# Latent attention: scores of both heads in row groups, value product in one piece, five turned pieces

## The chip, the core and the metric

The kernel runs on one NeuronCore of a Trainium2 chip. The metric is device time in microseconds (us) of one execution, the median of several. TensorE (PE) multiplies and transposes into PSUM, eight banks of 512 f32 columns; VectorE (DVE) and ScalarE (ACT) read PSUM and write SBUF, GpSimd (POOL) works in SBUF, SyncE (SP) issues DMAs. Each engine follows its own list of instructions; semaphores join them.

## What is computed

Two transformer blocks. The change touches the second attention of the first block, the latent one. Eight heads (H_B = 8), each with 64 own query and key numbers and 32 rotary ones; the rotary keys kr are the same for all heads. 1024 queries, in tiles of 128, meet 1280 keys (256 of the context, 1024 own).

```python
def mla_attend(qn, qr, kn, kr, v):
    s = (jnp.einsum('bqhd,bkhd->bhqk', qn, kn) + jnp.einsum('bqhr,bkr->bhqk', qr, kr)) * MLA_SCALE
    p = jax.nn.softmax(s, axis=-1)
    return jnp.einsum('bhqk,bkhd->bqhd', p, v)
```

All of it is in f32.

## The kernel before

`first_attention` runs the stages one after the other: a window attention (`attend_pairs`, line 710 scores, 733 value products, 690 transposes), then `project_latent`, then `attend_latent`. The window attention already scores its two heads from 64-row halves of the array in turn.

`project_latent` goes through a list `uses` of products, one PSUM bank each, eight banks in turn: rotary queries (four banks, rotated by VectorE), values (10), rotary keys (3), keys (12), queries (8), rotary queries turned (8). A bank of keys or queries holds two heads, 64 rows each; ScalarE copies one half, VectorE the other, since the two heads' operands are laid out differently: `kT_b` and `qT_b` have 96 rows for an even head (own 0 to 63, rotary 64 to 95) and 128 for an odd one (rotary 0 to 31, zeros, own 64 to 127). Rotary keys are copied four times over, once for each pair of heads.

`attend_latent` has 64 steps, a head and a tile of 128 queries each; two steps are a pair (`Pair`, 32 of them). A step needs three score matmuls (512, 512 and 256 columns over all 1280 keys), a maximum (956), an exponential with sum (981), a reciprocal and a scaling (951, 952), ten transposes in pieces of 4, 4 and 2 (897), each piece copied out of PSUM by ScalarE (974), VectorE (961), ScalarE (985), and half of a pair's value product (911), whose result VectorE copies (965). Two heads' scores lie in PSUM at once, at columns 0 and 1280, up to bank 5; pieces take banks 5 and 6 in turn, the product bank 7. The order on each engine is written out: TensorE scores two steps ahead, and puts one part of a step's scores, a piece, the other part, a piece, half a value product and the last piece behind one another. Each wait is on a count of a semaphore.

SyncE loads `w_out` in two halves, the second when 16 pairs are mixed; GpSimd scales them.

Of the kernel before, what the change touches and what calls it, by code (L numbers as in the profile page):

```python
# [476 lines left out]
def project_latent(c, k, kr4, q_rope):  # L477
# [9 lines left out]
    by_act, by_dve = [], []  # L487
    for kind, *at in uses:
        by_act.append((by_act[-1] if by_act else 0) + (kind != "rotate" and (kind != "value" or at[0] % 2 == 0)))
        by_dve.append((by_dve[-1] if by_dve else 0) + (kind != "rotate" and (kind != "value" or at[0] % 2 == 1)))  # L490
# [3 lines left out]

    with nc.Block(no_gpsimd_drain=True) as block:  # L495
        @block.gpsimd
        def _(pool):
            nc.gpsimd.memset(q_rope[:, :, :, 0, 32:64], 0.0).then_inc(spread, 1)
            nc.gpsimd.memset(kr4[:, :, 32:64], 0.0).then_inc(spread, 1)
            for at in (0, 64):  # L500
                nc.gpsimd.tensor_copy(kr4[:, :, at:at + ROPE], k.kr_key[:, :, :]).then_inc(spread, 1)

        @block.tensor
        def _(pe):
            pe.wait_ge(k.up_in["q"], 16)
            for n, (kind, *at) in enumerate(uses):
                if n >= 8:
                    if uses[n - 8][0] == "rotate":
                        pe.wait_ge(rotated, uses[n - 8][1] + 2)
                    else:  # L510
                        pe.wait_ge(act_out, by_act[n - 8])
                        pe.wait_ge(dve_out, by_dve[n - 8])
# [5 lines left out]
                elif kind == "key_rope":  # L518
                    pe.wait_ge(spread, 4)
                    a, b = at[0]  # L520
                    for t in range(a // P, b // P):
                        last = nc.tensor.transpose(bank(n)[0:96, P * t - a:P * t - a + P], kr4[:, t, :], k.ident[:, :])
# [4 lines left out]
                elif kind == "query_rope":  # L527
                    i, a = at
                    pe.wait_ge(rotated, a // P + 4)
                    for t in range(4):  # L530
                        last = nc.tensor.transpose(bank(n)[0:96, P * t:P * t + P],
                                                   q_rope[:, a // P + t, i, :, :].rearrange("p s n -> p (s n)")[:, 0:96], k.ident[:, :])
# [11 lines left out]
        @block.scalar  # L544
        def _(act):
            for n, (kind, *at) in enumerate(uses):
                if kind == "rotate" or kind == "value" and at[0] % 2:
                    continue
                act.wait_ge(made, n + 1)
                if kind == "key_rope":  # L550
                    a, b = at[0]
                    src = bank(n)[0:64, 0:b - a].unsqueeze(1).to_broadcast([64, PAIRS, b - a])
                    ins = nc.scalar.activation(k.kT_b[0:64, 1:HB:2, a:b], src, ACT.Identity)
                elif kind == "query":
                    i, a = at
                    ins = nc.scalar.activation(k.qT_b[0:64, 2 * i, a:a + BANK], bank(n)[0:64, :], ACT.Identity, scale=SCALE)
                elif kind == "query_rope":
                    i, a = at
                    ins = nc.scalar.activation(k.qT_b[0:64, 2 * i + 1, a:a + BANK], bank(n)[0:64, :], ACT.Identity, scale=SCALE)
                elif kind == "key":  # L560
                    i, (a, b) = at
                    ins = nc.scalar.activation(k.kT_b[0:64, 2 * i, a:b], bank(n)[0:64, 0:b - a], ACT.Identity)
                else:
                    act.wait_ge(spread, 4)
                    ins = nc.scalar.activation(k.v_b[:, at[0], :], bank(n), ACT.Identity)
                ins.then_inc(act_out, 1)

        @block.vector
        def _(dve):
            step = Chain(dve, link)  # L570

            def rotate(n, t):
# [9 lines left out]
                for s in range(2):  # L582
# [3 lines left out]
                nc.vector.tensor_tensor(q_rope[:, t, :, :, 0:ROPE], out.rearrange("p (i s e) -> p i s e", i=PAIRS, s=2),  # L586
                                        k.tmp[:, 0:256].rearrange("p (i s e) -> p i s e", i=PAIRS, s=2), ALU.add).then_inc(rotated, 1)

            for n, (kind, *at) in enumerate(uses):
                if kind == "value" and at[0] % 2 == 0:  # L590
                    continue
                dve.wait_ge(made, n + 1)
                if kind == "rotate":
                    for t in (at[0], at[0] + 1):
                        rotate(n, t)
                    continue
                if kind == "key_rope":
                    a, b = at[0]
                    src = bank(n)[64:96, 0:b - a].unsqueeze(1).to_broadcast([32, PAIRS, b - a])
                    ins = nc.vector.tensor_copy(k.kT_b[64:96, 0:HB:2, a:b], src)  # L600
                elif kind == "query":
                    i, a = at
                    ins = nc.vector.tensor_scalar(k.qT_b[64:128, 2 * i + 1, a:a + BANK], bank(n)[64:128, :], SCALE, None, ALU.mult)
                elif kind == "query_rope":
                    i, a = at
                    ins = nc.vector.tensor_scalar(k.qT_b[64:96, 2 * i, a:a + BANK], bank(n)[64:96, :], SCALE, None, ALU.mult)
                elif kind == "key":
                    i, (a, b) = at
                    ins = nc.vector.tensor_copy(k.kT_b[64:128, 2 * i + 1, a:b], bank(n)[64:128, 0:b - a])
                else:  # L610
                    dve.wait_ge(spread, 4)
                    ins = nc.vector.tensor_copy(k.v_b[:, at[0], :], bank(n))
                ins.then_inc(dve_out, 1)
# [220 lines left out]
def attend_latent(c, k, name, heads, bufs, d):  # L834
# [6 lines left out]
    n, W, HALF = 2 * len(heads), NK * P, NK // 2  # L841
    TURN = 5

    def scores(u):
        return c.ps[:, W * (u % 2):W * (u % 2) + W]

    def cuts(u):
        at = W * (u % 2)
        edges = [at] + [b for b in range(0, 8 * BANK, BANK) if at < b < at + W] + [at + W]
        cuts = [(a - at, b - at) for a, b in zip(edges, edges[1:])]  # L850
        return (cuts[:2], cuts[2:]) if u % 2 == 0 else (cuts[1:], cuts[:1])

    def product(p):
        return c.bank(7, P)

    PART = ((0, 4), (4, 4), (8, 2))

    def turn_bank(u, i):
        at = BANK * (TURN + (3 * u + i) % 2)
        return c.ps[:, at:at + P * PART[i][1]]  # L860

    def turned_out(eng, u, i):
        if i == 1:
            eng.wait_ge(out_dve, u + 1)
        else:
            eng.wait_ge(out_act, 2 * u + (1 if i == 0 else 2))

    def place(u, i):
        a, m = PART[i]
        return probT[:, (u // 2) % 2, u % 2, P * a:P * (a + m)]  # L870

    with nc.Block(no_gpsimd_drain=True) as block:
        @block.sync
        def _(sp):
            sp.dma_start(k.w_out[0], d["w_out"][0]).then_inc(k.w_out_in[0], 16)
            sp.wait_ge(mixed, n // 4)
            sp.dma_start(k.w_out[1], d["w_out"][1]).then_inc(k.w_out_in[1], 16)
# [12 lines left out]
        def _(pe):  # L890
            def turn(u, i):
                g = 3 * u + i
                if g >= 2:
                    turned_out(pe, (g - 2) // 3, (g - 2) % 3)
                a, m = PART[i]
                for j in range(m):
                    last = nc.tensor.transpose(turn_bank(u, i)[:, P * j:P * j + P], prob[:, u % 3, P * (a + j):P * (a + j) + P],  # L897
                                               k.ident[:, :])
                last.then_inc(turned, 1)

            def mix(p, half):
                out = product(p)
                if half == 0:
                    for u in (2 * p, 2 * p + 1):
                        turned_out(pe, u, 1)
                        turned_out(pe, u, 2)
                    if p:
                        pe.wait_ge(taken, p)
                for j in range(HALF * half, HALF * half + HALF):
                    for e in range(2):  # L910
                        last = nc.tensor.matmul(out[64 * e:64 * e + 64, :], heads[p].values[e][j],
                                                probT[:, p % 2, e, P * j:P * j + P], start=j == 0, stop=j == NK - 1,
                                                skip_group_check=True)
                if half == 1:
                    last.then_inc(mixed, 1)

            def score(u, part):
                for a, b in cuts(u)[part]:
                    last = nc.tensor.matmul(scores(u)[:, a:b], heads[u // 2].q[u % 2], heads[u // 2].keys[u % 2][:, a:b],  # L919
                                            start=True, stop=True, skip_group_check=True)  # L920
                return last

            for s in range(-2, n + 2):
                u = s + 2
# [2968 lines left out]
```

## Time and profile before

| | us |
|---|---|
| median of 3 runs (3193.18 to 3194.04) | 3193.26 |
| profiled execution | 3194.05 |
| its span | 3192.3 |
| first attention | 240 to 384 |
| latent projections | 384 to 457 |
| latent attention | 457 to 763.5 |
| TensorE busy | 3034.3 |
| mean granted TensorE clock | 0.978 |

An f32 matmul appears in the profile as two instructions with a weight load each, a transpose as one. The recorded length of an instruction of TensorE reaches past the start of the next, so lengths are not prices: the price of one is the distance from its start to the next one's. The stages follow one another without overlap.

### The profile page before, as it was taken

To read this page: it belongs to the slowest core of one execution; us is meant where nothing else is said; L and a number is where in the kernel's file an instruction comes from. 1 tells how busy PE (TensorE), PEld (TensorE's weight loads), DVE (VectorE), ACT (ScalarE), POOL (GpSimd) and SP (SyncE) were. 2 spreads that over 40 slices of the span, in tenths; PEclk is the share of its full clock that TensorE was granted. 3 is DMA by queue.
4 is the path that set the end of the run, shared out by engine and by line. 5 is a ranking of instruction groups with operands and counts; after the bars stand their busy time and mean duration, and the time that the engine had idled before them with its cause. 6 is when DMAs were issued, how large, how long until landed. Compare 5 with 4: busy or idle time off the path is not lost. (4 is left out here: it accounts for less than half of the span.)

```text
span 3192.3 us, 36679 instructions
## 1 busy us (share of the span) xinstructions
PE 3034.3 (95%) x14372; PEld 1715.9 (54%) x14372; DVE 1539.7 (48%) x2538; ACT 808.6 (25%) x1656; POOL 836.3 (26%) x654
## 2 busy tenths in 40 slices
PE   7999999999959999799999999999999999999999
PEld 3456746665424444344456657444445666665444
DVE  2445547776451111524322465314758777775234
ACT  3226534443211111412212026211112222221001
POOL 0004401002000110023032115312616665551323
PEclk9999999999979999899999999999999999999999
DMA  7210000002197986500000130012211122117443
GB/s 298 79 53 29 1 27 1 28 1 82 72 377 290 339 333 215 199 28 36 33 21 29 54 139 2 34 40 79 109 50 66 53 79 80 73 46 290 161 131 135
DMA packets 72315, 334.54 MB, mean 105 GB/s; under 512 B 10960, under 2 KB 12497, under 8 KB 58321
## 3 DMA queue, kind: packets, MB, share of 16 engines
q1 hardware_dynamic: 67536, 315.42, 26.0%
q0 software_dynamic: 4608, 16.78, 2.1%
q8 instruction: 115, 1.88, 0.2%
q14 instruction: 56, 0.45, 0.0%
HBM read 283.92 MB, written 48.23 MB: 104 GB/s over the span
## 5 line engine op out<-in xcount | busy, mean ns | idle before, releaser
L3444 PE MATMUL banks<-down_ring,down_sums 128*128 128x512 f32 x440 | 191.1, 597 | 4.2 <-DVE down_ring L3471 4.2
L919 PE MATMUL banks<-kT_b,qT_b_and_w_out 128*128 128x512 f32 (+3 forms) x384 | 161.9, 532 | 4.3 <-PEq L495 2.5
L3146 PE MATMUL banks<-hT,ffn_raw 128*128 128x512 f32 x352 | 157.6, 601 | 2.4 <-PEq L2632 1.3
L329 PE MATMUL banks<-w_in,hT 128*128 128x512 f32 (+1 forms) x384 | 157.1, 567 | 1.2 <-PEq L157 1.2
L3262 DVE SCALAR_TENSOR_TENSOR ffn_acc<-ffn_u,s_ffn_taps,ffn_acc 128x1023 f32<-128x1023 f32 x88 | 132.5, 1516 | 30.4 <-ACT ffn_acc L3199 28.8
L803 POOL TENSOR_TENSOR prob<-prob,softmax_columns 128x640 f32<-128x640 f32 (+1 forms) x64 | 75.4, 1199 | 263.7 <-DVE softmax_columns L759 263.7
L3444 PEld LDWEIGHTS banks<-down_ring,down_sums 128*128 128x128 f32 x440 | 84.1, 191 | 110.9 <-issue 103.4
L1867 PE MATMUL banks<-hT,side_ring 128*128 128x512 f32 x256 | 126.6, 614 | 1.3 <-PEq L2419 1.3
L1514 PE MATMUL banks<-expert_wg,expert_xT 128*128 128x512 f32 x256 | 114.9, 603 | 2.3 <-ACT expert_xT L1551 1.7
L1593 DVE TENSOR_TENSOR expert_h<-banks,expert_silu 128x512 f32<-128x512 f32 x16 | 11.1, 691 | 219.4 <-ACT expert_silu L1560 219.4
L329 PEld LDWEIGHTS banks<-w_in,hT 128*128 128x128 f32 x384 | 71.9, 190 | 77.9 <-issue 77.9
L1530 PE MATMUL banks<-expert_wd,expert_hT 128*128 128x512 f32 x256 | 112.6, 592 | 1.2 <-DVE expert_y L1585 1.2
L1514 PE MATMUL banks<-expert_wu,expert_xT 128*128 128x512 f32 x256 | 112.5, 592 | 0.0
L956 DVE TENSOR_REDUCE softmax_columns_b<-banks 128x1 f32<-128x1280 f32 x64 | 95.4, 1490 | 35.3 <-PE banks L919 35.3
L3146 PEld LDWEIGHTS banks<-hT,ffn_raw 128*128 128x128 f32 x352 | 67.8, 193 | 79.8 <-issue 76.8
L981 ACT ACTIVATE prob_b<-banks,softmax_columns_b 128x1280 f32<-128x1280 f32 x64 | 85.0, 1327 | 99.7 <-DVE softmax_columns_b L956 99.7
L1491 POOL DMA_INDIRECT expert_sums<-expert_y,idxT x16 | 25.3, 1582 | 319.6 <-DVE expert_y L1585 319.6
L897 PE MATMUL banks<-ident,prob_b 128*128 128x128 f32 x640 | 104.6, 278 | 0.9 <-ACT probT_b L985 0.4
L897 PEld LDWEIGHTS banks<-ident,prob_b 128*128 128x128 f32 x640 | 76.4, 141 | 52.0 <-issue 44.8
L3164 PE MATMUL banks<-ffn_split_rows,ffn_split_sums 128*128 128x256 f32 x352 | 84.0, 380 | 2.6 <-ACT ffn_chain L3189 2.5
L3471 DVE TENSOR_TENSOR down_ring<-down_ring 128x512 f32<-128x512 f32 x49 | 39.4, 810 | 96.3 <-DMA down_ring<-in_w_down 95.8
L2742 PE MATMUL banks<-hT,gate_ring 128*128 128x512 f32 x192 | 85.1, 592 | 0.7 <-PEq L673 0.7
(636 smaller groups left out, 6122.8 us busy)
## 6 DMA issues: line engine op xcount, KB each, us to landing
down_ring<-in_w_down SPq DMA_DIRECT2D x132, 256.0 KB, 2.9
expert_wg<-in_w_gate SPq DMA_DIRECT2D x16, 2048.0 KB, 15.4
expert_wu<-in_w_up SPq DMA_DIRECT2D x16, 2048.0 KB, 20.7
expert_wd<-in_w_down SPq DMA_DIRECT2D x16, 2048.0 KB, 8.7
ffn_raw<-in_w_ffn SPq DMA_DIRECT2D x22, 1024.0 KB, 6.4
wmod_slab<-in_w_mod SPq DMA_DIRECT2D x6, 2048.0 KB, 8.1
act_rows<-ffn_acc SPq DMA_DIRECT2D x22, 512.0 KB, 2.7
act_rows<-act_rows SPq DMA_DIRECT2D x22, 512.0 KB, 8.4
```

What stands on the lines that cost most here:

```text
L329: last = nc.tensor.matmul(c.ps[:, base + a:base + b], h[:, q, :], k.w_in[i][:, q, 0:b - a], start=q == 0, stop=q == KD - 1)
L897: last = nc.tensor.transpose(turn_bank(u, i)[:, P * j:P * j + P], prob[:, u % 3, P * (a + j):P * (a + j) + P], k.ident[:, :])
L919: last = nc.tensor.matmul(scores(u)[:, a:b], heads[u // 2].q[u % 2], heads[u // 2].keys[u % 2][:, a:b], start=True, stop=True, skip_group_ ...
L956: nc.vector.reduce_max(st[:, 0, u % 2:u % 2 + 1], scores(u), AX.X, negate=True).then_inc(negmax, 1)
L981: nc.scalar.activation(prob[:, u % 3, :], scores(u), ACT.Exp, bias=st[:, 0, u % 2:u % 2 + 1], accum_out=st[:, 1, u % 2:u % 2 + 1]).then_in ...
L1514: last = nc.tensor.matmul(c.bank(b), xT[:, e % 2, q, :], w[e % 3][:, q, :], start=q == 0, stop=q == KD - 1)
L1530: last = nc.tensor.matmul(c.bank(5 + half), hT[:, f, :], wd[e % 3][:, f, BANK * half:BANK * half + BANK], start=f == 0, stop=f == KF - 1)
L1867: last = nc.tensor.matmul(self.c.bank(6 + half), self.ring[:, f % 2, q, :], self.hT[:, q, BANK * half:BANK * half + BANK], start=q == 0, s ...
L2742: last = nc.tensor.matmul(product(g, m), wt[:, q, :], b[:, q, :], start=q == 0 and m != 2, stop=q == kt(g) - 1, skip_group_check=True)
L3146: last = nc.tensor.matmul(c.bank(fi), wt[:, q, :], x[:, q, :], start=q == 0 and m != 2, stop=q == 3, skip_group_check=True)
L3262: nc.vector.scalar_tensor_tensor(acc[:, fi, g, j:SEQ], u[:, g, fi, 0:SEQ - j], k.ffn_taps[:, (f * 2 + g) * 4 + 2 - j:(f * 2 + g) * 4 + 3 - j],
L3444: return nc.tensor.matmul(c.bank(4 * (p % 2) + t), stationary_of(s)[:, P * t:P * t + P], w[s % RING][:, 0, :], start=j == 0, stop=j == N - 1)
```

## The change

Scores are made for a pair of heads at once. `kT_b` now holds a pair's keys in 128 rows (64 each); the rotary keys lie once in `kr_b`, repeated in four groups of 32 rows, and the rotary queries of both heads twice over in the same way (the rotation's last step writes them doubled, POOL writes the keys fourfold). `score(p)` makes ten matmuls of 64 rows and 256 columns, heads in turn, and ten of 32 rows that add the rotary part, in three rounds. Head e has banks 3e to 3e+2, so PSUM holds the scores of one pair; five pieces of four transposes go through the two banks left (7, 6, 7, 6, 7), and the value product uses bank 6 as well. `prob` has two buffers of a pair instead of three of a head. In TensorE's order the scores of pair p+1 are followed by the value product of pair p-1 and then the five pieces of pair p. In the projections every bank is copied whole, ScalarE and VectorE in turn.

The core of the diff (lines removed are those of the functions printed above):

```diff
@@ project_latent @@
+            nc.gpsimd.tensor_copy(kr4[:, :, :, :], k.kr_key[:, :, :].unsqueeze(2).to_broadcast([P, NK, 4, ROPE])).then_inc(spread, 1)
...
@@ ScalarE (VectorE from first + 1) @@
+            for n in range(first, len(uses), 2):
                 act.wait_ge(made, n + 1)
+                out, src = out_of(n)
+                nc.scalar.activation(out, src, ACT.Identity, scale=SCALE if uses[n][0] in ("query", "query_rope") else 1.0).then_inc(act_out, 1)
...
+                twice = lambda x: x.rearrange("p (h e) -> p h e", h=HB).unsqueeze(2).to_broadcast([P, HB, 2, ROPE])
+                nc.vector.tensor_tensor(q_rope[:, t, :, :, :], twice(out), twice(k.tmp[:, 0:256]), ALU.add).then_inc(rotated, 1)
@@ attend_latent @@
+    n, W, CUT = len(heads), NK * P, BANK // 2
+    TURN = 6
+    PIECES = 5
+    ON_ACT, ON_DVE = {0: 1, 2: 2, 4: 3}, {1: 1, 3: 2}
...
-            sp.wait_ge(mixed, n // 4)
+            sp.wait_ge(mixed, n // 2)
...
+            def score(p):
+                if p:
+                    pe.wait_ge(exped, 2 * p)
+                qn, qr = heads[p].q
+                kn, kr = heads[p].keys
+                for a in range(0, W, CUT):
+                    for e in range(2):
+                        half = slice(64 * e, 64 * e + 64)
+                        nc.tensor.matmul(scores(e, a, CUT), qn[half, :], kn[half, a:a + CUT], start=a % BANK == 0, stop=False, skip_group_check=True)
+                for round_ in ((0, 512), (256, 768), (1024,)):
+                    for e in range(2):
+                        for i, a in enumerate(round_):
+                            rows = slice(64 * e + 32 * i, 64 * e + 32 * i + 32)
+                            last = nc.tensor.matmul(scores(e, a, CUT), qr[rows, :], kr[rows, a:a + CUT], start=False, stop=True, skip_group_check=True)
+                last.then_inc(scored, 1)
+            def turn(p, i):
+                if i == 0:
+                    pe.wait_ge(evened, 2 * p + 1)
+                    if p:
+                        pe.wait_ge(out_act, 3 * (p - 1) + ON_ACT[4])
+                elif i == 1:
                     if p:
                         pe.wait_ge(taken, p)
+                elif i == 2:
+                    pe.wait_ge(evened, 2 * p + 2)
+                    pe.wait_ge(out_act, 3 * p + ON_ACT[0])
+                elif i == 3:
+                    pe.wait_ge(out_dve, 2 * p + ON_DVE[1])
+                else:
+                    pe.wait_ge(out_act, 3 * p + ON_ACT[2])
+                for j in range(4):
+                    e, t = divmod(4 * i + j, NK)
+                    last = nc.tensor.transpose(turn_bank(i)[:, P * j:P * j + P], prob[:, p % 2, e, P * t:P * t + P], k.ident[:, :])
+                last.then_inc(turned, 1)
+            def mix(p):
+                pe.wait_ge(out_act, 3 * p + ON_ACT[4])
+                pe.wait_ge(out_dve, 2 * p + ON_DVE[3])
...
+            score(0)
+            for p in range(n):
+                if p + 1 < n:
+                    score(p + 1)
+                if p:
+                    mix(p - 1)
+                turn(p, 0)
...
+                turn(p, 4)
+            mix(n - 1)
...
@@ VectorE @@
+            for p in range(n):
+                if p + 1 < n:
+                    maxima(p + 1)
+                if p:
+                    take(p - 1)
+                turned_out(p, 1)
+                if p + 1 < n:
+                    even(p + 1, 0)
+                turned_out(p, 3)
+                if p + 1 < n:
+                    even(p + 1, 1)
+            take(n - 1)
...
@@ ScalarE @@
+            for p in range(n):
+                if p + 1 < n:
+                    exponents(p + 1, 0)
+                turned_out(p, 0)
+                if p + 1 < n:
+                    exponents(p + 1, 1)
+                turned_out(p, 2)
+                turned_out(p, 4)
```

`maxima`, `even`, `take`, `exponents` and `turned_out` are the reduction, the reciprocal with the scaling, the copy of the product, the exponential, and the copy of a piece, each for a pair's head or piece; `exponents(p, 0)` waits from the third pair on for the pieces of pair p-2, and each piece's copy for the product of pair p-2.

## Rows read from the trace of the kernel before

**Rows 1.** The page's busy times: us (share of the span) and instructions.

```profile
PE 3034.3 (95%) x14372; PEld 1715.9 (54%) x14372; DVE 1539.7 (48%) x2538; ACT 808.6 (25%) x1656; POOL 836.3 (26%) x654
```

**Rows 2.** Stretches: first attention, first scores, steady part, one pair of heads.

```profile
240.00:384.00 144.00, 135.96 (x1352) 102.34 (x1352) 80.29 (x216) 87.14 (x225) 75.41 (x64) 0.98 0.05 17
457.10:464.80 7.70, 7.28 (x10) 3.20 (x10) 1.50 (x2) 1.42 (x2) 0.00 (x0) 0.58 0.74 272
464.80:751.60 286.80, 285.00 (x2169) 194.50 (x2170) 204.66 (x278) 140.80 (x247) 20.38 (x8) 1.00 0.02 9
560.00:569.28 9.28, 9.28 (x74) 6.38 (x73) 6.47 (x10) 4.58 (x8) 0.00 (x0) 1.00 0.01 2
```

**Rows 3.** Waits, 465 to 751 us: us in total, times, longest us.

```profile
PEld banks L919 <- ACT prob_b L981: 2.5, 4, 1.3
```

**Rows 4.** Timeline of the latent attention: start us, us, instructions [idle before <-releaser].

```profile
562.83 1.88 PE L919 MATMUL banks<-kT_b,qT_b_and_w_out 128*128 128x512 f32 x4
...
564.15 0.89 DVE L952 TENSOR_SCALAR prob_b<-prob_b,softmax_columns_b 128x1280 f32<-128x1280 f32 x1
564.55 0.60 PE L897 MATMUL banks<-ident,prob_b 128*128 128x128 f32 x4
...
564.98 0.60 PE L919 MATMUL banks<-kT_b,qT_b_and_w_out 128*128 128x256 f32 x2
565.18 0.60 ACT L974 ACTIVATE probT_b<-banks 128x512 f32<-128x512 f32 x1 [0.99 <-PE banks L897]
...
565.42 0.60 PE L897 MATMUL banks<-ident,prob_b 128*128 128x128 f32 x4
565.62 1.49 DVE L956 TENSOR_REDUCE softmax_columns_b<-banks 128x1 f32<-128x1280 f32 x1 [0.58 <-PE banks L919]
...
565.95 1.31 PE L911 MATMUL banks<-probT_b,v_b 128*64 128x128 f32 x20
567.03 0.68 DVE L961 COPY probT_b<-banks 128x512 f32<-128x512 f32 x1
567.14 1.33 ACT L981 ACTIVATE prob_b<-banks,softmax_columns_b 128x1280 f32<-128x1280 f32 x1 [1.36 <-DVE softmax_columns_b L956]
...
567.19 0.44 PE L897 MATMUL banks<-ident,prob_b 128*128 128x128 f32 x2
...
567.47 1.88 PE L919 MATMUL banks<-kT_b,qT_b_and_w_out 96*128 96x512 f32 x4
```

**Rows 5.** Timeline of the first attention, by narrow windows.

```profile
302.19 1.31 PE L690 MATMUL banks<-ident,prob 128*128 128x128 f32 x10
303.43 0.49 PE L710 MATMUL banks<-kT_a,qT_a 64*128 64x256 f32 x2
...
303.75 0.60 PE L710 MATMUL banks<-kT_a,qT_a 64*128 64x256 f32 x4
...
303.97 0.60 PE L710 MATMUL banks<-kT_a,qT_a 64*128 64x256 f32 x4
...
304.24 0.59 ACT L809 ACTIVATE probT<-banks 128x512 f32<-128x512 f32 x1
...
304.88 0.20 PEld L733 LDWEIGHTS banks<-probT,v_a 128*64 128x64 f32 x4 [0.28 <-ACT probT L809]
```

**Rows 6.** Projections: timeline, and one group by line (busy us, mean ns).

```profile
385.75 0.84 POOL L501 COPY key_rope<-kr_key 128x320 f32<-128x320 f32 x2
...
L586 DVE TENSOR_TENSOR query_rope<-tmp 128x256 f32<-128x256 f32 x8 | 3.4, 425 | 0.3
...
451.88 4.91 DVE L606 TENSOR_SCALAR qT_b_and_w_out<-banks 32x512 f32<-32x512 f32 x8
...
453.79 0.93 PE L531 MATMUL banks<-ident,query_rope 128*96 128x128 f32 x7
```

**Rows 7.** Timeline: first scores, last product out.

```profile
457.18 7.28 PE L919 MATMUL banks<-kT_b,qT_b_and_w_out 96*128 96x512 f32 x10 [2.45 <-PEq L495]
...
763.19 0.29 DVE L965 COPY OT<-banks 128x128 f32<-128x128 f32 x1 [3.15 <-PE banks L911]
```

More of the change, by code:

```diff
@@ L486, in project_latent, with out_of @@
             + [("query_rope", i, a) for i in range(PAIRS) for a in (0, 512)])
[L487 to L490, printed above, removed]
+    first = NT // 2
     def bank(n):
         return c.bank(n % 8)
+    def out_of(n):
+        kind, *at = uses[n]
+        if kind == "value":
+            return k.v_b[:, at[0], :], bank(n)
+        if kind == "key_rope" or kind == "key":
+            a, b = at[-1]
+            return (k.kr_b[:, a:b] if kind == "key_rope" else k.kT_b[:, at[0], a:b]), bank(n)[:, 0:b - a]
+        i, a = at
+        return k.qT_b[:, 2 * i + (kind == "query_rope"), a:a + BANK], bank(n)
     with nc.Block(no_gpsimd_drain=True) as block:
@@ L497, in _ @@
         def _(pool):
[L498 to L501, printed above, removed]
+            nc.gpsimd.tensor_copy(kr4[:, :, :, :], k.kr_key[:, :, :].unsqueeze(2).to_broadcast([P, NK, 4, ROPE])).then_inc(spread, 1)
         @block.tensor
@@ L507, in _ @@
                 if n >= 8:
-                    if uses[n - 8][0] == "rotate":
-                        pe.wait_ge(rotated, uses[n - 8][1] + 2)
-                    else:
-                        pe.wait_ge(act_out, by_act[n - 8])
-                        pe.wait_ge(dve_out, by_dve[n - 8])
+                    before = n - 8 - first
+                    if before < 0:
+                        pe.wait_ge(rotated, 2 * (n - 8) + 2)
+                    elif before % 2 == 0:
+                        pe.wait_ge(act_out, before // 2 + 1)
+                    else:
+                        pe.wait_ge(dve_out, before // 2 + 1)
                 if kind == "rotate":
@@ L518, in _ @@
                 elif kind == "key_rope":
-                    pe.wait_ge(spread, 4)
+                    pe.wait_ge(spread, 1)
                     a, b = at[0]
                     for t in range(a // P, b // P):
-                        last = nc.tensor.transpose(bank(n)[0:96, P * t - a:P * t - a + P], kr4[:, t, :], k.ident[:, :])
+                        last = nc.tensor.transpose(bank(n)[:, P * t - a:P * t - a + P], kr4[:, t, :, :].rearrange("p g n -> p (g n)"), k.ident[:, :])
                 elif kind == "query":
@@ L530, in _ @@
                     for t in range(4):
-                        last = nc.tensor.transpose(bank(n)[0:96, P * t:P * t + P],
-                                                   q_rope[:, a // P + t, i, :, :].rearrange("p s n -> p (s n)")[:, 0:96], k.ident[:, :])
+                        last = nc.tensor.transpose(bank(n)[:, P * t:P * t + P], q_rope[:, a // P + t, 2 * i:2 * i + 2, :, :].rearrange("p h g n -> p (h g n)"),
+                                                   k.ident[:, :])
                 elif kind == "key":
@@ L545, in _ @@
         def _(act):
-            for n, (kind, *at) in enumerate(uses):
-                if kind == "rotate" or kind == "value" and at[0] % 2:
-                    continue
+            act.wait_ge(spread, 1)
+            for n in range(first, len(uses), 2):
                 act.wait_ge(made, n + 1)
[L550 to L566, printed above, removed]
+                out, src = out_of(n)
+                nc.scalar.activation(out, src, ACT.Identity, scale=SCALE if uses[n][0] in ("query", "query_rope") else 1.0).then_inc(act_out, 1)
         @block.vector
@@ new lines, in rotate @@
+                twice = lambda x: x.rearrange("p (h e) -> p h e", h=HB).unsqueeze(2).to_broadcast([P, HB, 2, ROPE])
+                nc.vector.tensor_tensor(q_rope[:, t, :, :, :], twice(out), twice(k.tmp[:, 0:256]), ALU.add).then_inc(rotated, 1)
+            for n in range(first):
+                dve.wait_ge(made, n + 1)
+                for t in (2 * n, 2 * n + 1):
+                    rotate(n, t)
+            dve.wait_ge(spread, 1)
+            for n in range(first + 1, len(uses), 2):
+                dve.wait_ge(made, n + 1)
+                out, src = out_of(n)
+                if uses[n][0] in ("query", "query_rope"):
+                    ins = nc.vector.tensor_scalar(out, src, SCALE, None, ALU.mult)
+                else:
+                    ins = nc.vector.tensor_copy(out, src)
@@ L840, in attend_latent, with scores, turn_bank, product @@
     prob, probT, col = bufs
[L841 to L870, printed above, removed]
+    n, W, CUT = len(heads), NK * P, BANK // 2
+    TURN = 6
+    PIECES = 5
+    ON_ACT, ON_DVE = {0: 1, 2: 2, 4: 3}, {1: 1, 3: 2}
+    def scores(e, a=0, m=W):
+        return c.ps[:, 3 * BANK * e + a:3 * BANK * e + a + m]
+    def turn_bank(i):
+        return c.bank(TURN + (1, 0, 1, 0, 1)[i])
+    def product():
+        return c.bank(TURN, P)
+    def place(p, i):
+        return probT[:, p % 2, BANK * i:BANK * i + BANK]
     with nc.Block(no_gpsimd_drain=True) as block:
@@ L890, in _ @@
         def _(pe):
[L891 to L906, printed above, removed]
+            def score(p):
[13 more added lines that the diff above has]
+                last.then_inc(scored, 1)
@@ L910, in mix @@
+            def mix(p):
+                pe.wait_ge(out_act, 3 * p + ON_ACT[4])
+                pe.wait_ge(out_dve, 2 * p + ON_DVE[3])
+                for j in range(NK):
                     for e in range(2):
-                        last = nc.tensor.matmul(out[64 * e:64 * e + 64, :], heads[p].values[e][j],
-                                                probT[:, p % 2, e, P * j:P * j + P], start=j == 0, stop=j == NK - 1,
+                        last = nc.tensor.matmul(product()[64 * e:64 * e + 64, :], heads[p].values[e][j],
+                                                probT[:, p % 2, P * (NK * e + j):P * (NK * e + j) + P], start=j == 0, stop=j == NK - 1,
@@ L913, in mix @@
                                                 skip_group_check=True)
[L914 to L924, printed above, removed]
-                if u < n:
-                    if u >= 2:
-                        pe.wait_ge(exped, u - 1)
-                    score(u, 0)
-                if 0 <= s < n:
-                    pe.wait_ge(evened, s + 1)
-                    turn(s, 0)
-                if u < n:
-                    if u:
-                        pe.wait_ge(exped, u)
-                    score(u, 1).then_inc(scored, 1)
-                if 0 <= s < n:
-                    turn(s, 1)
-                if s >= 2:
-                    mix(s // 2 - 1, s % 2)
-                if 0 <= s < n:
-                    turn(s, 2)
+                last.then_inc(mixed, 1)
@@ L943, in _ @@
+            score(0)
[5 more added lines that the diff above has]
+                turn(p, 0)
+                turn(p, 1)
+                turn(p, 2)
+                turn(p, 3)
+                turn(p, 4)
+            mix(n - 1)
         @block.vector
@@ L945, in _ @@
             step = Chain(dve, link)
-            for s in range(-2, n + 2):
-                u = s + 2
-                if 0 <= u - 1 < n:
-                    st = col[:, (u - 1) // 2 % 4, :, (u - 1) % 2:(u - 1) % 2 + 1]
-                    dve.wait_ge(exped, u)
-                    step(nc.vector.reciprocal(st[:, 2, :], st[:, 1, :]))
-                    nc.vector.tensor_scalar(prob[:, (u - 1) % 3, :], prob[:, (u - 1) % 3, :], st[:, 2, :], None, ALU.mult).then_inc(evened, 1)
-                if u < n:
-                    st = col[:, (u // 2) % 4]
-                    dve.wait_ge(scored, u + 1)
-                    nc.vector.reduce_max(st[:, 0, u % 2:u % 2 + 1], scores(u), AX.X, negate=True).then_inc(negmax, 1)
-                if 0 <= s < n:
-                    dve.wait_ge(turned, 3 * s + 2)
-                    if s >= 4:
-                        dve.wait_ge(mixed, s // 2 - 1)
-                    nc.vector.tensor_copy(place(s, 1), turn_bank(s, 1)).then_inc(out_dve, 1)
-                if s >= 3 and s % 2 == 1:
-                    p = s // 2 - 1
-                    dve.wait_ge(mixed, p + 1)
-                    nc.vector.tensor_copy(heads[p].out, product(p)).then_inc(taken, 1)
@@ new lines, in maxima, with even @@
+            def maxima(p):
+                dve.wait_ge(scored, p + 1)
+                for e in range(2):
+                    nc.vector.reduce_max(col[:, p % 4, 0, e:e + 1], scores(e), AX.X, negate=True).then_inc(negmax, 1)
+            def even(p, e):
+                dve.wait_ge(exped, 2 * p + e + 1)
+                st = col[:, p % 4, :, e:e + 1]
+                step(nc.vector.reciprocal(st[:, 2, :], st[:, 1, :]))
+                nc.vector.tensor_scalar(prob[:, p % 2, e, :], prob[:, p % 2, e, :], st[:, 2, :], None, ALU.mult).then_inc(evened, 1)
@@ new lines, in turned_out, with take @@
+            def turned_out(p, i):
+                dve.wait_ge(turned, PIECES * p + i + 1)
+                if i == 1 and p >= 2:
+                    dve.wait_ge(mixed, p - 1)
+                nc.vector.tensor_copy(place(p, i), turn_bank(i)).then_inc(out_dve, 1)
+            def take(p):
+                dve.wait_ge(mixed, p + 1)
+                nc.vector.tensor_copy(heads[p].out, product()).then_inc(taken, 1)
+            maxima(0)
+            even(0, 0)
+            even(0, 1)
+            for p in range(n):
[9 more added lines that the diff above has]
+                    even(p + 1, 1)
@@ new lines, in turned_out @@
+            def turned_out(p, i):
+                act.wait_ge(turned, PIECES * p + i + 1)
+                if i == 0 and p >= 2:
+                    act.wait_ge(mixed, p - 1)
+                nc.scalar.activation(place(p, i), turn_bank(i), ACT.Identity).then_inc(out_act, 1)
+            exponents(0, 0)
+            exponents(0, 1)
+            for p in range(n):
[6 more added lines that the diff above has]
+                turned_out(p, 4)
```

62 lines of the change are left out of this document (12 added, 50 removed).

## The prediction

> **What bounds the kernel now.** I read the table of stages first, then the waits of the latent attention, then its timeline. TensorE is busy 95% of the span [rows 1], and no other engine over 48%. In the steady stretch of the latent attention it is busy 285.0 of 286.8 us at full clock, VectorE 204.7 and ScalarE 140.8 [rows 2]; the longest wait of TensorE there sums to 2.5 us [rows 3]. So this stage goes as fast as TensorE's list of instructions, and the change must be costed there, with the question whether TensorE still never waits.
>
> One head is the stretch from 562.83 to 567.47 [rows 4], start to start: four score instructions of 512 columns 1.72 us, four transposes 0.43, two score instructions of 256 columns 0.44, four transposes 0.53, twenty value instructions 1.24, two transposes 0.28. The sum is 4.64 us, so a pair of heads takes 9.28. Each f32 matmul is two instructions (six for a head's three matmuls), a transpose is one. The unit prices are thus 0.215 us for 256 columns, 0.109 for a transpose and 0.109 for two value instructions, which run side by side because the heads use different 64-column halves. Going from full-array work into the halves and back costs 0.10 (0.53 against 0.43) + 0.15 (1.24 against 1.09) + 0.06 (0.28 against 0.22) = 0.31, of which 0.09 to 0.10 is the gap at each switch and 0.05 the slower first instruction.
>
> **The change, part by part.** Scores: ten matmuls of 64 rows (20 instructions of 256 columns) alternate between the heads, then ten of 32 rows (20 more) bring the rotary part in three rounds; four row groups are used in two rounds and two in the last. The nearest row for two row groups is the first attention, which scores both heads so: the first two instructions lie within 0.49 us, the second two start at 303.75 and the third two at 303.97 [rows 5]. So two groups do run side by side, at 0.215 for a pair, and neither pass of a matmul holds up the other group: in strict order with both passes together the first instruction would have stood alone. The first pair takes 0.32, 0.10 more, and before it the transposes end with a gap (302.19 to 303.43 is 1.24 for ten). Ten pairs cost 0.32 + 9 x 0.215 = 2.26, and 0.09 for each switch.
>
> Rotary part: no row shows four groups. From below it is what four abreast cost, 3 rounds x 2 passes = 6 slots: 0.32 + 5 x 0.215 = 1.40. Two abreast it is 10 slots, 2.26, as the 64-row part. One at a time it would be 20 slots, 4.4, and 96 us over the stage; [rows 5] exclude that for two groups, so I leave it out of the range. I take 1.40: two groups were wholly independent in [rows 5], and two more differ from them in nothing that a row shows. The Trainium skill (TensorE: Matmul & The Clock Gate, Measured speedup vs the span model) gives 3.07x, not 4x, for four row groups of 32; by that the four-slot part of the rounds, 0.86, would be 1.12, an estimate. No run here shows it. The same notes (TensorEngine Tiling (Array Packing), Key Properties) say that changing the tiling mode drains the engine; the trace agrees, with the gaps of 0.09 above, and a pair now has four such changes (transposes, 64 rows, 32 rows, column halves) where it also had four.
>
> Value product: the same 40 instructions of a pair, now in one piece: 1.24 + 10 x 0.109 = 2.33 with its exit. Transposes: the same 20, 2.18 + 0.06 + 0.09 = 2.33. TensorE's own list is then 2.26 + 0.09 + 1.40 + 0.09 + 2.33 + 2.33 = 8.50 us, 0.78 less than 9.28. That is the gain, if nothing waits.
>
> Waits: before, a single head's scores had a buffer of their own, and TensorE always had other work. Now six banks hold one pair, two are left for all turned pieces and the product, and the product shares a bank with pieces 1 and 3. I lay out one round, with 0 where VectorE sees the scores of the next pair. A signal is seen 0.20 after TensorE is free (next matmul 565.42, reduce 565.62; 564.98 and the copy at 565.18 alike) [rows 4], and TensorE sees a copy's end after 0.05 (304.24 + 0.59 against 304.88) [rows 5].
>
> - TensorE: free at -0.20, value product from -0.11, transposes of piece 0 from 2.22 to 2.72.
> - VectorE: the two maxima, 1.49 each, with 0.08 of overlap, to 2.90; only then the product's copy, 0.28, to 3.10. Piece 1 needs its bank: it starts at 3.15 instead of 2.72 and ends at 3.65 (0.06 + 0.44 after each pause).
> - ScalarE: first exponential 1.52 to 2.85; copy of piece 0 (0.60) from 2.92 to 3.52; second exponential, behind it, 3.48 to 4.80; copy of piece 2, behind that, to 5.40.
> - TensorE: piece 2 without a pause to 4.09; piece 3 waits for VectorE's copy of piece 1 (3.85 + 0.68 = 4.53), 4.58 to 5.08; piece 4 waits for ScalarE's copy of piece 2 and runs from 5.45 to 5.95.
>
> Then the next scores: 0.09 + 2.26 + 0.09 + 1.40 + 0.20 = 4.04, so the round closes at 9.99. The exponentials that the scores wait for were over at 4.9. The three pauses are 0.43 + 0.49 + 0.37 = 1.29, with their restarts 1.47: 0.78 is gained and 1.47 given back, 0.7 lost for a pair. Behind the held transposes in TensorE's queue stand the next scores, for which both maxima and exponentials wait. The scaling of the rows by VectorE (0.89 a head [rows 4], and a reciprocal) ends before 8 and is not late.
>
> Projections: the wide copies replace half-height ones and are dealt out in turn. TensorE's list is the same. The eight 32-row copies of VectorE end at 456.79 although TensorE's last transpose is over at 454.72 [rows 6]; with four each they end near 455.5, so the attention starts 1.3 us sooner. The rotation's last step writes twice as much, 0.42 to some 0.68, eight times: 2.1 us of VectorE, whose next job is a copy of values with banks to spare under 17 us of matmuls. The new POOL copy of 1280 elements is about four times the 0.42 of one copy of 320 [rows 6], done 24 us before it is read. Both cost nothing in time. The second load of w_out waits for the same pair, the 16th, and nothing on its queue is earlier.
>
> Ends: the first scores start after a pause, at half clock (7.70 us at a mean of 0.58) [rows 2, 7]. New: first scores 0.32 + 15 slots at 0.43 and gaps, about 7.3, signal at 463.4; maxima and exponentials 4.4 with TensorE idle; second scores 3.84 at full or 7.5 at half clock. Their signal comes at 471.8 to 475.7, or 3.3 earlier if the shorter pause keeps the clock; I take 472. Thirty rounds of 9.98: 771.4. After it the pieces, the product (2.3), the last pieces without an exponential but with the same two-bank waits, and the last product add 15.2: 786.6, against 763.5 [rows 7]. That is +23.1.
>
> The profiled execution is 3194.05 us for a span of 3192.3; the median of the runs is 3193.26. Nothing after the stage changes, so 3193.3 + 23.1 = 3216.4.
>
> **Rivals.**
>
> - Two abreast: the rotary groups share something, or the two passes of one matmul take the slots in order. For: no row with four. Against: the independence in [rows 5]. +0.86 for each of 32 pairs, +27.5: 3244. From about 3237 up this one holds.
> - Dearer rounds: four abreast, but each of the four full slots half as long again, midway between the bounds: 4 x 0.108 = 0.43, x 32 = 14: 3230. By the 3.07x of the page above it would be 0.26 x 32 = 8 and 3225, an estimate.
> - Faster: the pauses don't bind. For: by their sums VectorE (6.47 of 9.28) and ScalarE (4.58) have room [rows 2]. Against: the order of their queues, which the round above lays out. If ScalarE and VectorE freed both banks as fast as TensorE turns, the round would be 8.50: 0.78 x 32 = 25 less, of which the slower start of one pair at a time takes 3 back: 3171. It decides once the pauses come under 0.78 together, half of what I find.
> - Clock: the pauses could lower the granted clock. In the first attention TensorE is idle 8 of 144 us in short pieces at 0.98 [rows 2]; here 1.5 of 10, none over 0.6. A half clock for a tenth of the stage costs 15 us. Unlikely.
>
> **Numbers.** Forecast 0.62; dearer rounds 0.12; two abreast 0.12; faster 0.09; clock and what I have not thought of 0.05. A measurement tells 0.2%, 6.4 us, from no change. Faster 0.09, within 0.2% 0.04 (a forecast whose pauses are half as long), slower 0.87. The forecast's own range is 3208 to 3226: the switch into 32 rows, which no row shows, costs between nothing and twice the 0.19 of the switch into 64 rows, so 0.19 x 32 = 6 either way, and the start is uncertain by 3. The range, taking in two abreast, is 3205 to 3245.
>
> **What would show it.** The 32-row instructions start four within some 0.02 us, rounds 0.215 apart; a pair takes 9.98 us; TensorE waits three times a round, for the copy of the product, for VectorE's copy of piece 1 and for ScalarE's copy of piece 2; the stage spans about 456 to 787. I am wrong if pieces 1, 3 and 4 follow without pauses, or if the 32-row groups queue up behind each other.

## The result and the profile after

The changed kernel takes 3219.45 us in the median (3217.97 to 3222.14, four runs) against 3193.22 before (3192.12 to 3194.04): ratio 1.008, 95% interval 1.0066 to 1.0093, slower by 26.2 us. The forecast was 3216.4.

A round is the work on one pair of heads in the steady part, from one start of the 32-row scores to the next. Shown are the page's busy times of the changed kernel, then two stretches of its latent attention: 29 rounds, and one of them.

```profile
PE 3035.5 (94%) x15268; PEld 1748.7 (54%) x15268; DVE 1520.9 (47%) x2522; ACT 791.1 (25%) x1609; POOL 832.3 (26%) x651
```

```profile
480.98:768.66 287.68, 267.91 (x2902) 209.56 (x2900) 185.38 (x261) 125.31 (x203) 21.05 (x8) 1.00 0.02 9
600.02:609.94 9.92, 9.24 (x102) 7.22 (x101) 6.29 (x9) 4.32 (x7) 0.00 (x0) 1.00 0.01 2
```

The 287.68 us are 29 rounds of 9.92 us (9.28 before [rows 2, 4]), at full clock. TensorE is idle in 19.8 of them; before it was idle 1.8 of 286.8. Its busy time over the whole kernel hardly moved (3034.3 before [rows 1]), although the list is shorter: a recorded length reaches past the next start, and before a pause it reaches into the pause. In the round shown the pauses cost 1.4 by the starts below, and only 0.68 are recorded as idle. So the list and the pauses are read from the distances of starts, and the causes of the pauses from the waits.

The waits of TensorE's matmuls (PE) and weight loads (PEld) for other engines, 480 to 770 us: us in total, times, longest us.

```profile
PE banks L888 <- DVE probT_b L933: 8.5, 29, 0.3
PE banks L888 <- DVE OT L937: 7.6, 29, 0.3
```

```profile
PEld banks L888 <- DVE probT_b L933: 15.4, 29, 0.5
PEld banks L888 <- DVE OT L937: 14.5, 29, 0.5
PEld banks L888 <- ACT probT_b L968: 10.5, 29, 0.4
```

Each occurs 29 times, once a round: transposes (line 888) wait for VectorE's copy of a piece, for its copy of the product and for ScalarE's copy of a piece. [rows 3] had one wait, of four times. The timeline of one round has them in place.

```profile
600.02 1.57 PE L868 MATMUL banks<-kr_b,qT_b_and_w_out 32*128 32x256 f32 x20
...
601.52 2.40 PE L896 MATMUL banks<-probT_b,v_b 128*64 128x128 f32 x40
601.63 2.89 DVE L921 TENSOR_REDUCE softmax_columns_b<-banks 128x1 f32<-128x1280 f32 x2 [2.81 <-PE banks L868]
603.22 1.33 ACT L961 ACTIVATE prob_b<-banks,softmax_columns_b 128x1280 f32<-128x1280 f32 x1 [4.85 <-DVE softmax_columns_b L921]
...
603.86 0.65 PE L888 MATMUL banks<-ident,prob_b 128*128 128x128 f32 x4
604.44 0.28 DVE L937 COPY OT<-banks 128x128 f32<-128x128 f32 x1
...
604.55 0.60 ACT L968 ACTIVATE probT_b<-banks 128x512 f32<-128x512 f32 x1
...
604.78 1.15 PE L888 MATMUL banks<-ident,prob_b 128*128 128x128 f32 x8 [0.26 <-DVE OT L937]
605.04 1.32 ACT L961 ACTIVATE prob_b<-banks,softmax_columns_b 128x1280 f32<-128x1280 f32 x1
605.47 0.69 DVE L933 COPY probT_b<-banks 128x512 f32<-128x512 f32 x1 [0.75 <-PE banks L888]
...
606.22 1.44 PE L888 MATMUL banks<-ident,prob_b 128*128 128x128 f32 x8 [0.29 <-DVE probT_b L933]
...
606.35 0.60 ACT L968 ACTIVATE probT_b<-banks 128x512 f32<-128x512 f32 x1
...
607.58 2.43 PE L863 MATMUL banks<-kT_b,qT_b_and_w_out 64*128 64x256 f32 x20
...
609.94 1.35 PE L868 MATMUL banks<-kr_b,qT_b_and_w_out 32*128 32x256 f32 x18
```

Start to start: 32-row scores 1.50, value product 2.34, pieces 3.72, 64-row scores 2.36. Without pauses the pieces would take 2.33, so the pauses cost 1.4. Piece 1 starts at 604.78 although piece 0 is over at 604.35 (four times 0.109 and 0.06 after 603.86): the product's bank is copied at 604.44, behind both maxima. Piece 3 starts at 606.22, after VectorE's copy of piece 1 (605.47 + 0.69). Piece 4 is inside the last group; ScalarE's copy of piece 2 stands behind the second exponential and ends at 606.95.

Two narrow windows of the same stretch show how the 32-row scores run.

```profile
600.02 0.50 PE L868 MATMUL banks<-kr_b,qT_b_and_w_out 32*128 32x256 f32 x4
...
600.34 0.61 PE L868 MATMUL banks<-kr_b,qT_b_and_w_out 32*128 32x256 f32 x8
```

Four instructions start within 0.02 us of each other and together last 0.50 us, and the next eight, two sets of four, lie within 0.61. Two row groups had 0.49 and 0.60 for the same [rows 5].

### The profile page after: what moved, and what is told of

It reads as the page before. It is cut to its first block and busy times, and to the rows that moved or that the text cites. A ratio compares the mean times of both kernels' runs of the same rounds, so it can differ in the third digit from the quotient of the medians.

```text
span 3216.4 us, 38252 instructions
## 1 busy us (share of the span) xinstructions
PE 3035.5 (94%) x15268; PEld 1748.7 (54%) x15268; DVE 1520.9 (47%) x2522; ACT 791.1 (25%) x1609; POOL 832.3 (26%) x651
## 5 line engine op out<-in xcount | busy, mean ns | idle before, releaser
L888 PEld LDWEIGHTS banks<-ident,prob_b 128*128 128x128 f32 x640 | 67.3, 141 | 54.3 <-DVE probT_b L933 15.9
L863 PE MATMUL banks<-kT_b,qT_b_and_w_out 64*128 64x256 f32 x640 | 81.1, 399 | 5.4 <-ACT prob_b L961 4.4
```

The lines of the kernel that those rows point to most:

```text
L888: last = nc.tensor.transpose(turn_bank(i)[:, P * j:P * j + P], prob[:, p % 2, e, P * t:P * t + P], k.ident[:, :])
```

## Experiments

All were built from the changed kernel. Ratios are to the kernel before the change, run beside them (3193.29 in the first four, 3194.74 in the last three; 3193.22 for the changed kernel above). Differences to the changed kernel are taken from its round where the totals are too near to each other. The round given is the median distance between starts of the 32-row scores.

**Rotary part on two row groups.**

```diff
-                            rows = slice(64 * e + 32 * i, 64 * e + 32 * i + 32)
+                            rows = slice(64 * e, 64 * e + 32)
```

> Both rotary matmuls of a head use the same 32 rows, so that only two row groups run side by side; the sum is the same, because the four groups hold the same numbers. If the groups run independently and the scores lie on the path that closes the round, the full rounds take twice as long: 0.86 us more for each of 32 pairs, +27, 3246. Rival: the pauses of TensorE in the pieces take it up, or four groups were not worth more than two: within 3 of 3219.

3248.34 us (1.0182, 1.0165 to 1.0199), round 10.88. The 32-row scores, 1.50 before, now are 2.46 from start to start:

```profile
600.65 2.53 PE L868 MATMUL banks<-kr_b,qT_b_and_w_out 32*128 32x256 f32 x20
...
603.11 2.40 PE L896 MATMUL banks<-probT_b,v_b 128*64 128x128 f32 x40
```

So all of it lands in the time, 0.96 a round; the pauses absorb nothing, since the scores and the pauses lie one after the other. It is 0.10 more than expected: in the second half of the list the two instructions of a pair start 0.11 apart instead of together, and the last one ends so much later. Four abreast is worth 29 us here.

**Maxima and exponentials cut to a tenth.**

```diff
-                    nc.vector.reduce_max(col[:, p % 4, 0, e:e + 1], scores(e), AX.X, negate=True).then_inc(negmax, 1)
+                    nc.vector.reduce_max(col[:, p % 4, 0, e:e + 1], scores(e, 0, W if p < 2 else P), AX.X, negate=True).then_inc(negmax, 1)
...
-                nc.scalar.activation(prob[:, p % 2, e, :], scores(e), ACT.Exp, bias=col[:, p % 4, 0, e:e + 1],
+                m = W if p < 2 else P
+                nc.scalar.activation(prob[:, p % 2, e, 0:m], scores(e, 0, m), ACT.Exp, bias=col[:, p % 4, 0, e:e + 1],
```

> From the third pair on the maxima and the exponentials cover 128 of 1280 keys; the rest of the probabilities is left as it stood, TensorE's list and all copies are the same. Two theories of the pauses. One: two banks for five pieces. A bank is free again 0.20 + 0.60 + 0.05 after its last transpose, the other piece covers 0.44 of that, so two pauses stay however idle the other engines are: the pieces end at 5.42 instead of 5.95 in a round, 9.4 us a round, 3203. The other: the copies stand behind maxima and exponentials in the queues of VectorE and ScalarE. With these short nothing pauses, the round is TensorE's list of 8.5: 3174.

3209.13 us (1.0057, 1.0041 to 1.0074), round 9.53. The pieces still pause twice:

```profile
607.02 1.12 PE L888 MATMUL banks<-ident,prob_b 128*128 128x128 f32 x8
608.46 1.12 PE L888 MATMUL banks<-ident,prob_b 128*128 128x128 f32 x8 [0.32 <-ACT probT_b L969]
609.77 0.66 PE L888 MATMUL banks<-ident,prob_b 128*128 128x128 f32 x4 [0.19 <-ACT probT_b L969]
610.36 2.43 PE L863 MATMUL banks<-kT_b,qT_b_and_w_out 64*128 64x256 f32 x20
```

Two pieces, a pause, two pieces, a pause, one piece. Of the 1.4 that the pauses cost, 1.0 stays, although the maxima and exponentials are nearly gone; the scaling of whole rows and the copies stay as they were. In the round's own time the pieces end at 5.47 (5.42 expected). The gain of 0.39 a round is less than the expected 0.53 for two reasons: the pieces of the changed kernel end at 5.86 and not at the 5.95 from which the gain was counted, and the first of the two pauses is 0.50 instead of 0.41 (the second is 0.37). Why piece 2 starts 0.14 after the end of the copy that it waits for, and not 0.05, stays open.

**Four banks for the pieces and the product.**

```diff
-        return c.ps[:, 3 * BANK * e + a:3 * BANK * e + a + m]
+        return c.ps[:, 2 * BANK * e + a % 1024:2 * BANK * e + a % 1024 + m]
+
+    def read(e):
+        return c.ps[:, 2 * BANK * e:2 * BANK * e + CUT].unsqueeze(1).to_broadcast([P, 5, CUT])
...
-        return c.bank(TURN + (1, 0, 1, 0, 1)[i])
+        return c.bank((7, 6, 5, 7, 6)[i])
...
-        return c.bank(TURN, P)
+        return c.bank(4, P)
```

with the maxima and exponentials reading `read(e)`, and the waits changed to fit the banks. This kernel does not compute the attention any more; it is built only to price the banks.

> The scores of the last 256 keys are added onto those of the first 256, and maxima and exponentials read these first 256 columns five times over instead of 1280 different ones: same instructions and sizes, but the scores take four banks, and four are left: three for pieces in turn, one for the product. The order on every engine is the same. If banks are the cause, pieces run without pause to about 4.5; then the scores wait for the second exponential until 4.95, so a round is 8.8 and the time about 3186, under the kernel before the change. If the order of the queues is the cause, banks change little: above 3210.

3184.96 us (0.9972, 0.996 to 0.9984), round 8.85. The twenty transposes of a pair are one group:

```profile
607.86 2.54 PE L883 MATMUL banks<-ident,prob_b 128*128 128x128 f32 x20
...
610.51 0.92 PE L866 MATMUL banks<-kT_b,qT_b_and_w_out 64*128 64x256 f32 x6
```

The weight load at the start of the scores, a round earlier, shows what the scores wait for:

```profile
601.67 2.03 PEld L866 LDWEIGHTS banks<-kT_b,qT_b_and_w_out 64*128 64x128 f32 x20 [0.35 <-ACT prob_b L958]
```

The instructions, their sizes and their order are the same on every engine, and the two maxima and the exponential take as long as before (2.89 and 1.33). So the banks alone turn 26 us slower into 8 faster. What is left is a short wait of the scores for the second exponential, as expected.

**Piece 0 ahead of the value product.**

```diff
-        return c.bank(TURN + (1, 0, 1, 0, 1)[i])
+        return c.bank((7, 7, 6, 7, 6)[i])
...
+                turn(p, 0)
                 if p:
                     mix(p - 1)
-                turn(p, 0)
```

with both exponentials behind the copy of piece 0 on ScalarE.

> Piece 0 goes ahead of the value product, and its bank takes piece 1 too: banks 7, 7, 6, 7, 6. ScalarE copies it before the first maximum is out, so both exponentials follow each other, and the copy of the product comes before TensorE needs its bank. Costs two more switches, 0.31. By my chart the pieces end at 5.41 instead of 5.95 with the switches counted: round 9.4, 3203, still slower than the kernel before the change. Rival: each of the three later pieces waits for a copy as before, and the switches come on top: 3225 or more.

3204.08 us (1.0039, 1.0025 to 1.0054), round 9.44, as charted. An order that fits two banks better wins back 0.48 a round, though it adds two switches, but two pauses stay: before piece 3, for VectorE's copy of piece 1, and before piece 4, inside the second group, for ScalarE's copy of piece 2.

```profile
607.23 1.18 PE L892 MATMUL banks<-ident,prob_b 128*128 128x128 f32 x8
608.67 1.29 PE L892 MATMUL banks<-ident,prob_b 128*128 128x128 f32 x8 [0.26 <-DVE probT_b L937]
609.29 0.42 PEld L892 LDWEIGHTS banks<-ident,prob_b 128*128 128x128 f32 x4 [0.21 <-ACT probT_b L972]
```

**A third bank, borrowed from the scores.** On top of the run before:

```diff
-        return c.bank((7, 7, 6, 7, 6)[i])
+        return c.bank((7, 7, 2, 6, 7)[i])
...
                 for a in range(0, W, CUT):
+                    if a == 2 * BANK and p >= 2:
+                        copied(p - 2, 2)
...
                 elif i == 2:
+                    pe.wait_ge(exped, min(2 * p + 3, 2 * n))
+                elif i == 3:
```

VectorE also copies piece 3 ahead of the first scaling instead of behind it, which the run before does not. No pause of that run waits for the copy of piece 3, so the gain is put down to the bank; the order by itself was not run.

> The order of the run with piece 0 first, and piece 2 in bank 2, which is free between the first exponential (2.9 in the round) and the last 64-row score matmul of the next pair. Banks 7, 7, 2, 6, 7. Nothing is left out. If banks are the cause, pieces 2, 3 and 4 follow without pauses, the pieces end at 4.69 instead of 5.41, the exponentials are over at 4.35, and a round is 8.7: 3181, 12 under the kernel before the change. If only a bank for the product, or shorter queues, counted in the run with four banks, this one stays at 3200.

3182.09 us (0.9962, 0.9948 to 0.9975), round 8.81 (8.7 expected), and it computes everything. The pauses of the pieces are gone, and the round is TensorE's list, 8.50 + 0.31 for the two switches:

```profile
601.29 1.57 PE L876 MATMUL banks<-kr_b,qT_b_and_w_out 32*128 32x256 f32 x20
602.79 0.66 PE L896 MATMUL banks<-ident,prob_b 128*128 128x128 f32 x4
603.38 2.40 PE L904 MATMUL banks<-probT_b,v_b 128*64 128x128 f32 x40
605.72 2.10 PE L896 MATMUL banks<-ident,prob_b 128*128 128x128 f32 x16
607.74 2.43 PE L871 MATMUL banks<-kT_b,qT_b_and_w_out 64*128 64x256 f32 x20
```

**Copy of piece 2 on VectorE.**

```diff
-    ON_ACT, ON_DVE = {0: 1, 2: 2, 4: 3}, {1: 1, 3: 2}
+    ON_ACT, ON_DVE = {0: 1, 3: 2, 4: 3}, {1: 1, 2: 2}
```

> Only the copy of piece 2 moves from ScalarE, where it stands behind the second exponential, to VectorE, behind the copy of piece 1; ScalarE takes piece 3. Order and banks as in the changed kernel. Chart: copy of piece 2 from 4.53 to 5.21 instead of 4.80 to 5.40, piece 4 ends at 5.76 instead of 5.95: 6 less, 3213. If the second exponential were what holds the round, the gain would be up to its whole pause of 0.37 a round, 3207.

3216.01 us (1.006, 1.0044 to 1.0075). The interval overlaps that of the changed kernel, so the total does not show the gain; the round does, 9.74: 0.18 less, where the chart has 0.19. When ScalarE's exponential is out of the way of piece 2, VectorE's queue takes its place.

**A filled wait at the start.**

```diff
             score(0)
+            for j in range(40):
+                nc.tensor.transpose(turn_bank(j % 2)[:, 0:P], k.ident[:, :], k.ident[:, :])
```

> Forty transposes of the identity, 4.4 us, whose results nobody reads, fill TensorE's wait between the first and the second scores; all else as in the changed kernel. The second scores ran at half clock there (4.64 instead of 2.43 for the 64-row part), the third partly. If the idle time before them is why, they run at full clock and the time is 4 less, 3215. If the clock falls anyway, 3219.

3217.15 us (1.0067, 1.0052 to 1.0082): the interval reaches the changed kernel's, so the total tells nothing. The timelines do. From the first scores of the changed kernel:

```profile
456.57 2.43 PE L863 MATMUL banks<-kT_b,qT_b_and_w_out 64*128 64x256 f32 x20 [0.99 <-PEq L502]
458.93 1.57 PE L868 MATMUL banks<-kr_b,qT_b_and_w_out 32*128 32x256 f32 x20
464.93 4.64 PE L863 MATMUL banks<-kT_b,qT_b_and_w_out 64*128 64x256 f32 x20 [4.43 <-ACT prob_b L961]
469.50 1.59 PE L868 MATMUL banks<-kr_b,qT_b_and_w_out 32*128 32x256 f32 x20
471.03 1.09 PE L888 MATMUL banks<-ident,prob_b 128*128 128x128 f32 x8
474.72 1.06 PE L888 MATMUL banks<-ident,prob_b 128*128 128x128 f32 x8 [2.60 <-ACT probT_b L968]
476.42 1.12 PE L888 MATMUL banks<-ident,prob_b 128*128 128x128 f32 x4 [0.64 <-ACT probT_b L968]
477.47 3.58 PE L863 MATMUL banks<-kT_b,qT_b_and_w_out 64*128 64x256 f32 x20
```

And of the run with the filled wait:

```profile
455.47 2.43 PE L863 MATMUL banks<-kT_b,qT_b_and_w_out 64*128 64x256 f32 x20 [0.99 <-PEq L502]
...
463.85 2.43 PE L863 MATMUL banks<-kT_b,qT_b_and_w_out 64*128 64x256 f32 x20
...
474.08 3.67 PE L863 MATMUL banks<-kT_b,qT_b_and_w_out 64*128 64x256 f32 x20
```

The second 64-row scores go at full clock, 2.43 instead of 4.64, when TensorE was kept busy before them; the third are slow in both, after the pauses of 2.6 and 0.6 us between the first pieces. From first to third scores it is 18.61 instead of 20.90 us: 2.3 gained, not 4.

## Why the prediction was right, point by point

**TensorE's list.** Right. 64-row scores with their switch 2.36 (2.35 forecast), 32-row scores 1.50 (1.49), value product 2.34 (2.33). The list is 8.5, and the run with a third bank attains it with its two more switches, 8.81.

**Four row groups.** Right, and the rival with two abreast is refuted twice: by the sets of four in the trace, and by the run with two groups, which costs 29 us. Sets of four follow one another at 0.215 us, as pairs do, so the rival of dearer rounds falls too. The 3.07x that the Trainium skill gives for four row groups at 512 columns (TensorE: Matmul & The Clock Gate, Measured speedup vs the span model) would make that distance longer, and is not borne out in it here.

**The pauses.** Right in place and number: three in a round, 29 times each. In the round's own time, from 601.63, piece 1 starts at 3.15 (3.15 forecast), piece 3 at 4.59 (4.58), and the pieces end 0.09 before 607.58, at 5.86 (5.95). The difference is ScalarE's second exponential, which began at 3.41, not 3.48. The round is 9.92 against 9.98, and the rival of a lower clock falls with it: the granted clock is 1.00 over the 29 rounds, in spite of the pauses. My reason in the text was the order of the queues and the two banks together. The runs weigh them: short queues alone give back 0.39 of the 1.4 that the pauses cost, banks alone 1.07. The remaining 0.35 with four banks is a wait for the second exponential.

**Projections.** The forecast had the attention start 1.3 us sooner. In the profile shown it started only 0.6 sooner, at 456.57 (457.18 before [rows 7]), but the projections had begun 0.9 later. The first lines of the projections, before and after:

```profile
384.58 10.60 PE L516 MATMUL banks<-w_q_up,cqT 128*128 128x256 f32 x48 [0.74 <-PEq L673]
```

```profile
385.44 10.60 PE L522 MATMUL banks<-w_q_up,cqT 128*128 128x256 f32 x48 [0.73 <-PEq L651]
```

From there to the first scores it is 72.6 us before and 71.1 in the changed kernel and in all seven runs: 1.5 less. All of it lies in the pause ahead of the first scores, 0.99 instead of 2.45.

**Ends.** Several terms were wrong and cancel, which is luck. I charged the first scores half clock (7.3 us); they took 3.9 at full clock, after a pause of TensorE of 1.0 us instead of 2.5 [rows 7]. My 472 for the second scores counted them at full clock (3.84); they took 6.1, since their 64-row part ran at half clock. So they were seen at 471.1 after all. The third scores ran partly at half clock, which I did not charge: the first round took 11.45 instead of 9.98. The 29 rounds after it gave 1.7 back, and what follows the last scores took 15.9 instead of 15.2. The last product is out at 786.15 (786.6 forecast).

**Sum.** The stage ends 22.7 us later than before (23.1 forecast), but 0.9 of that arose before the projections, where nothing was changed; their first product starts between 384.3 and 386.3 in the profiles of the changed kernel and the seven runs. The changed stages alone cost 21.8: 1.5 gained in the projections and 23.3 lost in the attention, where 1.3 and 24.4 were forecast. The medians differ by 26.2. The 4.4 between are the 0.9 ahead of the stages, 1.4 behind them, and 2.1 because the profiled execution is 1.3 below its median and the one before the change 0.8 above its own. Where the 0.9 and the 1.4 come from stays open. So the forecast was 1.3 too high for the stages, and its total 3 too low.

**The rival on the other side** (faster, pauses don't bind, 3171) fell for the kernel as changed, but what it describes exists: with a third bank the same scores come to 3182, with 0.31 more of switches in each round.

## What to carry to other kernels

Packing small matmuls into row groups can keep its promise to the hundredth of a microsecond and still lose, when its results need more of PSUM at once. Before putting pieces behind one another, divide the time for which a bank is held by the number of banks. Here it is held for 0.44 of writing, 0.20 until the copy starts, 0.60 of copying and 0.05 until TensorE goes on, 1.29 together: with two banks that is 0.65 for a piece that needs 0.44. The run with short maxima and exponentials, where the copies that TensorE waited for found their engine free, came near it, with 1.44 and 1.31 for two pieces. A bank whose contents have been read, and which is written late in the next step, serves in between: with one, the reordered kernel went from 0.4% slower to 0.4% faster.

## What was not expected of the hardware

Four row groups cost no more than two: 32-row sets of four follow at 0.215 us, and the four instructions of a set start within 0.02 us (0.50 for all four, where two took 0.49 [rows 5]).

In these traces the clock fell after the long pauses of TensorE and not after the short ones. After 1.0 us without work the first scores ran at 2.4 GHz (granted clock 1.00); after 2.5 us, in the kernel before, they began at 1.2 GHz (0.50). After 4.4 us the 64-row part of the second scores ran at 1.2 GHz (0.50) and the 32-row part behind it at 2.4 GHz (0.97). The third scores began at 1.2 GHz again (0.50), after two more pauses, of 2.6 and 0.6 us. In the run with a third bank these pauses were 0.7 and 1.2 us, and the third scores ran at 2.4 GHz throughout (1.00), although the slow stretch of the second scores had lasted longer there, with 2.29 for their 32-row part.
